# Products ahead of the last value products, evictions signalled by bank, and logits within the convolution's value product

## The reference, cut to what matters

```python
def window_attention(q, k, v, k_ctx, v_ctx, sink):      # layer 2 of the first block
    ...
o = window_attention(q, k, v, k_c, v_c, sink_logit[i])
y = (o * jax.nn.silu(g)) @ w_out_c[i]                    # "co"
x = x + gate * y
...
def fox_attention(q, k, v, log_f):                       # causal, 8 heads of 64
    cum = jnp.cumsum(log_f, axis=1)
    ...
def hybrid_mixer(h, w_in, b_f, conv_w, conv_b, conv_ln_g, conv_ln_b, w_o):
    proj = h @ w_in                                      # "b2": q2, k2, v2, f, cv, cg
    q, k, v, f_logit, conv_val, conv_gate = jnp.split(proj, splits, axis=-1)
    log_f = jax.nn.log_sigmoid((f_logit + b_f).astype(jnp.float32))
    attn = fox_attention(q, k, v, log_f)
    u = conv_val * jax.nn.sigmoid(conv_gate)
    u = causal_depthwise_conv(u, conv_w, conv_b)         # 31 taps, 512 channels
    u = jax.nn.silu(layer_norm_2(u, conv_ln_g, conv_ln_b))
    return jnp.concatenate([attn, u], axis=-1) @ w_o     # "wo"

def swiglu_ffn(h, w_ffn_in, w_ffn_out):                  # "fi" and "fo"
    g, u = jnp.split(h @ w_ffn_in, 2, axis=-1)
    return (jax.nn.silu(g) * u) @ w_ffn_out
```

## Time and profile before

| | us |
|---|---|
| median of 3 runs | 2482.07 |
| lowest, highest | 2478.64, 2483.53 |
| profiled execution | 2482.6 |
| its span | 2480.7 |
| PE busy (share) | 2305.7 (93%) |
| POOL busy | 1393.0 (56%) |
| DVE busy | 1442.4 (58%) |
| ACT busy | 773.6 (31%) |
| mean granted clock of PE | 0.968 |

### The profile page before, as it was taken

One profiled execution on the slowest core, in us unless ns is written; L12 is line 12 of the kernel. 1 busy time (PEld: TensorE's weight loads), 2 busy tenths in 40 slices (PEclk: granted clock), 3 DMA queues, 4 the chain that ended last, 5 costly groups with the idle time before them and its releaser, 6 DMA issues. The chain is left out here.

```text
span 2480.7 us, 32206 instructions
## 1 busy us (share of the span) xinstructions
PE 2305.7 (93%) x11283; PEld 1901.0 (77%) x11283; DVE 1442.4 (58%) x2162; ACT 773.6 (31%) x1405; POOL 1393.0 (56%) x1372
## 2 busy tenths in 40 slices
PE   6898999999999999989978988899999999999995
PEld 2778889888887877867756767787788888888874
DVE  1753665678782899957778968858612222221236
ACT  3321112223221788833333248724210000000012
POOL 2537555755985788547679643376755633333360
PEclk9899999999999899989989989999999999999997
DMA  8436345414566655352233575552222211111121
GB/s 279 151 94 197 110 133 170 178 53 152 161 200 183 183 167 162 94 182 85 56 120 106 161 174 168 146 215 88 92 76 78 93 51 52 45 45 47 52 68 68
DMA packets 180446, 305.92 MB, mean 123 GB/s; under 512 B 34940, under 2 KB 73528, under 8 KB 179008
## 3 DMA queue, kind: packets, MB, share of 16 engines
q1 hardware_dynamic: 140512, 222.75, 30.6%
q10 hardware_dynamic: 39776, 81.12, 8.9%
HBM read 247.14 MB, written 56.66 MB: 122 GB/s over the span
## 5 line engine op out<-in xcount | busy, mean ns | idle before, releaser
L1162 PE MATMUL PS<-HXH,WH 128*128 128x512 f32 (+1 forms) x1904 | 758.2, 398 | 57.2 <-POOL WL L1046 10.2
L1043 POOL TENSOR_SCALAR WH<-RAW 128x512 fp32r<-128x512 f32 (+1 forms) x466 | 338.9, 727 | 773.5 <-PE PS L1164 637.7
L1164 PE MATMUL PS<-HXH,WL 128*128 128x512 f32 (+1 forms) x1904 | 750.0, 394 | 0.0
L1163 PE MATMUL PS<-HXL,WH 128*128 128x512 f32 (+1 forms) x1904 | 749.9, 394 | 0.0
L1046 POOL TENSOR_TENSOR WL<-RAW,WH 128x512 fp32r<-128x512 f32 (+1 forms) x466 | 633.5, 1359 | 39.0
L1162 PEld LDWEIGHTS PS<-HXH,WH 128*128 128x128 f32 (+1 forms) x1904 | 361.2, 190 | 144.4 <-issue 12.8
L1164 PEld LDWEIGHTS PS<-HXH,WL 128*128 128x128 f32 (+1 forms) x1904 | 360.4, 189 | 79.8 <-issue 2.1
L1163 PEld LDWEIGHTS PS<-HXL,WH 128*128 128x128 f32 (+1 forms) x1904 | 361.2, 190 | 78.8 <-issue 3.6
L2427 DVE TENSOR_TENSOR TM<-PS,TM 128x512 f32<-128x512 f32 x44 | 28.4, 686 | 365.8 <-ACT TM L1846 365.8
L1846 ACT ACTIVATE TM<-PS 128x512 f32<-128x512 f32 x44 | 23.9, 596 | 550.5 <-PE PS L1164 550.4
L2440 DVE TENSOR_TENSOR Y<-PS,Y 128x2048 f32<-128x2048 f32 x40 | 91.7, 2292 | 116.9 <-PE PS L1164 116.8
(11 more groups left out here) (313 smaller groups left out, 4100.8 us busy)
## 6 DMA issues: line engine op xcount, KB each, us to landing
RAW<-in_ada_w SPq DMA_DIRECT2D x160, 256.0 KB, 2.8
RAW<-in_w_ffn_in SPq DMA_DIRECT2D x224, 128.0 KB, 2.1
RAW<-in_w_in_ab SPq DMA_DIRECT2D x88, 256.0 KB, 2.7
RAW<-in_w_in SPq DMA_DIRECT2D x56, 256.0 KB, 2.6
RAW<-in_w_ffn_out SPq DMA_DIRECT2D x56, 256.0 KB, 2.6
XR<-XX ACTq DMA_DIRECT2D x3, 4096.0 KB, 12.1
XX<-XR ACTq DMA_DIRECT2D x3, 4096.0 KB, 14.9
RAW<-in_w_in_c SPq DMA_DIRECT2D x40, 256.0 KB, 2.6
```

The lines of the kernel that those rows point to most:

```text
L1043: g.tensor_scalar(WH[:, sw, 0:m], RAW[:, r, 0:m], 1.0, 0.0, ALU.mult, ALU.add).then_inc(gpsimd_done, 1)
L1162: mm(out, wh, xh, start=first, stop=False, **kw)
L1163: mm(out, wh, xl, start=False, stop=False, **kw)
L1164: return mm(out, wl, xh, start=False, stop=last, **kw)
```

## The change

Six parts, by the names in the code:

1. *Evictions by bank.* PE signals `("jobb", name, j)` after the last product of each bank. ACT's evictions of the b2, wo and fi jobs and of the q and g jobs wait for their bank, and so does DVE's product in fi.
2. *Logits.* `flog`'s products are issued within cv h1, six behind each step's twelve. Their weights are one tile of 128 x 64 loaded in one transfer and split by two small instructions on POOL instead of sixteen. They go to banks 2 and 3 of the set that holds the convolution's sums; the sums that use these banks wait until DVE has read the logits. DVE's and ACT's steps on the logits stand where they stood.
3. *POOL's turns.* The adds of `conv(-2)` alternate with the splits for q2.
4. *Waits at the attentions.* PE's window attention waits only for set 0 and, at its first transposes (u = 5), for set 1; ACT's waits at both starts go. PE's causal attention waits by bank for its first two steps. The variance sums move to u = 2 of it and ACT's root to u = 3. DVE no longer waits for the root at the start. The stores of v2 h1's low parts move from ACT's queue to SP's, behind `load_qk(1)` and ahead of `load_v(0)`.
5. *Out-projections begin within the attentions.* Twelve products of co (0, h0), k = 0, are issued at u = 131 and 132, ahead of the last value products; twelve of wo (0, h0), k = 7, at u = 71 and 72. Wo's first job takes its steps in the order 7, 6, 5, 4, 0 to 3. ACT's and DVE's splits of the rows needed first (`high_rows`, `low_rows`) are issued at set steps of the attention. The gating of the last output block on DVE comes after the low rows of h0.
6. *The small sum.* `hload` of h1 moves on DVE behind the `adapost` for vector 8.

The diff, cut to its core:

```diff
-CONV_TAIL = (5, 7, 9, 11, 13, 15, 17, 19, 22)
+CONV_TAIL = (7, 9, 11, 13, 14, 15, 17, 19, 22)
+WO_FIRST = [7, 6, 5, 4, 0, 1, 2, 3]
...
+    ev("hload", ("hload", 1, "h0"), n=1, part="h0")
+    ev("reload", ("reload", 1), n=1)
...
                 ev("adapost", ("adapost", late, None), v=late, n=None)
+            if (g, p) == (0, "h0"):
+                ev("hload", ("hload", 1, "h1"), n=1, part="h1")
...
+            w_f = slot("split", ("b2", "f", 0), None)
...
         lin((name, p), "b2", name, p, w, last=True, midk=6,
+            mid=("stat", 2, "h1") if (name, p) == ("cv", "h0") else None, gates=w_f if (name, p) == ("cv", "h1") else None)
...
+            def store_v_low():
+                off = PARTS["h1"][0]
+                for j in range(4):
+                    sp.wait_ge(vector_done, upto("slo", ("v2", "h1"), j))
...
                 if f == 8:
-                    load_v(0)
                     load_qk(1)
                     load_nb(1)
+                    store_v_low()
+                    load_v(0)
                     load_v(1)
...
                                 ins = three(bank(name, j, n), WH[:, sw, ws], WL[:, sw, ws], xh, xl, f, l)
+                                if l and j < 3:
+                                    ins.then_inc(products_done, 1)
+                                    did(products_done, ("jobb", name, j))
...
+                        if e.get("gates") is not None:
+                            gate_logits(k, e["gates"])
...
                 elif kind == "attc":
-                    for job_before in prev[name]:
-                        pe.wait_ge(*of("free", job_before))
+                    pe.wait_ge(*of("free", prev[name][0]))
...
+                        if u == min(tiles):
+                            pe.wait_ge(*of("free", prev[name][1]))
...
+                        if u in CO_STARTS:
+                            if u == CO_STARTS[0]:
+                                pe.wait_ge(vector_done, upto("mx", "c", 127))
+                            lin_step(next(x for x in TL if x["name"] == ("co", 0, "h0")), 0,
+                                     (0, 1) if u == CO_STARTS[0] else (2, 3))
...
+                        if u == 2:
+                            conv_sums(("cvar", "x"))
...
-                            if u >= 2:
-
+                            if u < 2:
+                                pe.wait_ge(*of("freeb", prev[name][0], sb + 1))
+                            else:
...
+            CO_HIGH = {129: [0], 132: [1], 133: [2], 134: [3]}
+            WO_HIGH = {66: [7], 68: [6], 70: [5], 71: [4]}
...
+                    by_bank = layer in ("b2", "wo", "fi") or (layer == "c" and group[0] in "qg")
+                    if not by_bank:
+                        act.wait_ge(products_done, upto("job", name))
...
+                                act.wait_ge(products_done, upto("jobb", name, j))
                                 A(SPH[j][:, :], bank(name, j), ACT.Copy,
                                   scale=-SCALE if group == "q2" else 1.0).then_inc(scalar_done, 1)
...
+                        if u == 3:
+                            x = ("cvar", "x")
+                            act.wait_ge(products_done, upto("job", x))
...
+            CO_LOW = {129: [0], 133: [1], 134: [2, 3]}
+            WO_LOW = {71: [7], 72: [6], 73: [5, 4]}
...
+                            elif x:
+                                dve.wait_ge(vector_done, upto("free", "flog"))
...
-                    dve.wait_ge(scalar_done, upto("csd"))
```

219 lines of the change are left out of this document (146 added, 73 removed).

## The result

The changed kernel takes 2452.35 us (median of 4 runs, 2449.60 to 2453.65) against 2480.82 (median of 4, 2478.64 to 2483.53): a ratio of 0.9879, 95% interval 0.9865 to 0.9892, or 28.5 us less. The forecast was 2439 in a range of 2420 to 2460: the sign and the range hold, the size is off by a third (43 us were forecast off the profiled run, 29.3 came off its span, 2480.7 to 2451.4). The profiled execution took 2453.2 us.

The account below looks back on a forecast made before the run. PE was taken to bound the kernel, busy 93%, so only its idle time and the slow clock behind pauses could be bought. Terms summing to 43.4 us off the profiled 2482.6 gave 2439 us, range 2420 to 2460.

Parts of the forecast that it names:

- main case: Whole kernel: the summed terms give 2439 us, own range 2429 to 2450, chance 63%.
- first rival: Whole kernel: only the edges gain, convolution stage 0 to 4, causal attention nothing, 26 us in all, 2456; chance 18%.
- Co, 9.9 forecast: Out-projection behind the window attention: removed waits and slow starts give 12.7 us, less 2.8 for a new wait inside co(1,h0).
- The convolution stage, 14.3: Cg h1 through v2: logits inside the value product gain 5.8 us, q2, k2 and v2 starts by bank 8.5.
- S: Start of cv h1, 1230.45 before, from which the chain to q2 h0 was counted.
- The term for the alternate turns: Convolution stage: POOL's taps alternating with splits come 3.21 us apart; ACT's eight taps take 11.6, ending at 70.8 after cv h1's start.
- The causal attention, 3.5: Its start: scores ahead of variance sums start PE 7.1 us earlier, ACT's 3.7 eats half; 3.5, range 0 to 7.
- the rival which had the move of the stores to SP as a cost: Causal attention: v2 h1's low stores on SP delay head loads; at 8 us a head the kernel takes 2495; chance 6%.
- The recorded estimate of 2.1: Start of causal attention: gain if each table switch costs some 2.66 us, a load of 1.28 and a drain of 1.38.
- FFN and tail, 4.5: Last two FFN products' AHL waits, table load and clock give 4.0 us (2 to 6); small rests 0.5 (0 to 1).
- The window attention, 5.0: Its start: PE's 3.88 us wait for all of PSUM goes, with 1.1 of slow start; range 3.9 to 7.
- narrow waits bring nothing: Whole kernel: ACT and DVE are late by their own queues, so PE waits as long elsewhere; within 5 us; chance 4%.

Follow-up runs that it names:

- gate_first: Changed kernel, but DVE gates the last output block of the window attention ahead of the last four low rows of h0: 2446.29 us, ratio 0.9858.
- evicting first: Changed kernel, but DVE evicts co(0,h0) into XX ahead of the eight low rows of h1: 2446.87 us, ratio 0.9861.
- second profile of before: The kernel before, without an edit, run once more for another profile: 2474.43 us for this one execution.
- taps_in_row: Changed kernel with POOL's eight adds of conv(-2) in a row again, ahead of the splits for q2: 2450.93 us, ratio 0.9869 (two runs).
- Sums_first: Kernel with gating and eviction put first in co, variance sums and ACT's root back at the causal attention's first step, ahead of its scores: 2438.24 us, ratio 0.9835.
- Stores_on_act: Kernel with gating and eviction put first in co, the low stores of v2 h1 issued by ACT again: 2444.48 us, ratio 0.9857.
- both_first: Changed kernel with the last output's gating ahead of h0's last four low rows and co(0,h0)'s eviction ahead of h1's low rows: 2440.18 us, ratio 0.9835.
- wait_for_job: Changed kernel with every eviction by bank waiting for the end of the job again, the signals kept: 2471.12 us, ratio 0.9951.
- no_co_start: Changed kernel without the twelve products of co(0,h0) ahead of the last value products; rows still made early: 2446.69 us, ratio 0.9859.
- logits_alone: Kernel before with only the logits' products moved inside cv h1: 2480.37 us against 2485.14, ratio 0.9984.

## Why the prediction was right, and where it was not

The frame held: PE's idle places carried the argument, their removal made the kernel faster, and five of the nine stages behind the first row lie within 2 us of their terms. But the three largest misses all go one way, 17 us too much, and the measured 2452.35 is outside the main case's own range of 2429 to 2450. It lies in the stated range since that was drawn wide enough for most of the first rival. The sign was reasoned; that the time fell inside is in part luck, for 4.5 us came from places that I had priced at next to nothing.

Of the signs that I named, some failed. The logits are read 48.8 us after cv h1 starts (44 said), q2 h0 starts after 76.5 (73), v2 h0 after 169.5 (165). From the first score of the causal attention to the last value product it takes 152.9 us where it took 142.3, 10.6 longer and not 3 to 4. And one sign of being wrong came: the jobs from q2 h0 to v2 h0 take 23.2 us each, over 23, where PE alone would need 21.6.

**Co, 9.9 forecast, 1.3 measured.** The removed waits went as priced: counted from the window attention's last score PE was 6.3 us ahead at the end of co(0,h0) (1097.0 and 1087.7, less the 3.0) and 10.2 at the start of co(1,h0), where 6.4 and 10.1 were forecast. The failing step is the one that bounded the new wait by 1.7 to 4.7: it was 7.62. I had written that the gating stands behind low rows and costs up to 3. The store came 22.4 us after the last score and not 12.7 as before, 9.7 later. 5.4 of it go with the gating put first (17.0 in "gate_first"). The value products came later behind co's twelve, and the low rows doubled in length beside POOL's splits, 5.16 for four where 2.50 is the price without them. The eight rows of h1 took 10.51, where I had them end 33.6 us after the attention's last product by the row of 6.88 for six. "The transfer hangs on the attention's last rows as before" was the wrong half of a sentence whose other half named the danger. Gating first and evicting first give 5.9 and 7.9 alone and 11.6 together. Against the second profile of before, without the wait for MOD, the changed kernel's co stage is even 5.0 us longer (116.4 and 111.4): this part of the sum rested on a wait that one of three traces of this order doesn't have.

**The convolution stage, 14.3 and 10.1.** The chain was right in its order and wrong by two terms. Up to q2 h0 the stage gave 2.4 and not 5.8, behind it 7.7 and not 8.5. S moved 2.0 us earlier by its own term, but DVE did not move with it; I counted the logits' reading from S on both sides and so took these 2 us twice. And the XX scalings took 3 more us beside POOL's splits. Together the 5.0 by which the reading at S+48.8 is later than my S+43.8; a shorter chain behind it gave 1.6 back, and q2 h0 started at S+76.5, not S+73.1. The term for the alternate turns was sized rightly (3.17 a turn) and meant nothing, as "taps_in_row" shows: POOL's first split is as late.

**The causal attention, 3.5 and -0.8.** PE did begin 7.0 us earlier after v2 h1. The step that failed is that ACT's root eats half. PE's new waits for the root (2.15) and for the first values (1.81) take more than half, its waits for K are 4.1 us in all where they were 3.6, and the stage came out 0.8 longer. "Sums_first" shows that the earlier scores are worth nothing within 2 us. "Stores_on_act" shows, for the loads as they now stand, that the rival which had the move of the stores to SP as a cost had its sign wrong: it saves more issuing time on ACT than it costs in waits for loads. Against the kernel before, the start as a whole gained nothing. That only issuing time is saved by it, as the Trainium skill has it ("DMA: Bandwidth & Descriptors", Issuing engines are not separate DMA queues), the runs agree with: the last of these stores lands 17.1 us after the end of v2 h1 when SP issues them ("both_first") and 16.4 when ACT does; here the issuing alone is 4 us or more, because ACT's queue stood in front of the first exponential. The recorded estimate of 2.1 takes off one drain, though two table loads are added; in the changed kernel's trace the next ACTIVATE starts 1.29 us after each of the two loads (1450.70 and 1451.99, 1453.13 and 1454.42), so neither shows a drain.

**FFN and tail, 4.5 and 8.9** with wo's evictions. I priced only the last two waits, and 2.3 of the 4.4 above the forecast are wo's by "wait_for_job"; the rest lies in small waits of the FFN, each under 1.1 us, that I had rated at 0.5 together. The two AHL waits shrank by 1.44 and 1.94, as forecast.

**The window attention, 5.0 and 6.1.** PE starts at once. The slow start that went with the wait was larger than the 1.1 that I took from another place: the granted clock was 0.50 behind it. What PE meets instead at 811.17, 1.52 us for DVE's maxima behind ACT's first exponential, I had not seen; set 1 is free when it is asked for.

The rivals: "only the edges gain" (2456) is nearer to the measured time than the main case. It was right that the causal attention gives nothing and that the taps in turn hold ACT, and wrong on the convolution stage, which gave 10 us and not 0 to 4. That SP's queue makes the whole slower is refuted by "stores_on_act", for the loads as they now stand. That narrow waits bring nothing is refuted by "wait_for_job".

Open: why the rows of h1 take 16.8 us from issue to first landing in one execution of the kernel before and 14.3 in another (13.5 to 16.3 in the other kernels), and why the causal attention takes 133 to 138 us from first to last score in kernels that differ only ahead of it. Waits for K loads differ with it, but no run here separates them. The waits at the start of the window attention and the early start of wo were not undone alone, and "both_first" was not run without co's early products, so whether they would pay there is not shown.

## What to carry to other kernels

When work is pulled ahead of the end of a stage, ask what it frees: here twelve products stood ahead of the value products and let GpSimd start, which slowed VectorE; both delayed a store, and the earlier start cost 8 us in the traces (6 in the medians) where 6 were to be gained. A wait that is removed is worth what the next late thing on that path leaves: follow the transfer behind it to its issue, not from its landing. Signalling each bank instead of the job was the plain part and gave two thirds of the gain, because two engines then overlap on one set of buffers, also where the evicting engine is the one that is full. And before two traces are compared stage by stage, take off what they already differ by ahead of the first of these stages: here it was 3.2 us, as much as between two executions of one kernel.

## What the runs showed of the hardware

A subtraction of 128x512 with both inputs in SBUF took DVE 0.62 us on average with POOL idle ("no_co_start") and 1.29 beside POOL's splits (the changed kernel), and POOL's own two-input step went from 1.28 to 1.60. Eight XX scalings took 8.77 us in the kernel before, where the last four ran beside POOL's splits of the logits' small weights, and 11.70 in "logits_alone", where POOL splits weights of 128x512 beside them. Issuing four stores took ACT 7.24 us in "stores_on_act", with nothing computed meanwhile, and 4.83 in the kernel before. And one wait of 3.69 us with 2.6 of slow clock behind it came and went between executions of one binary, which moved it by some 6 us.
